# A two-block network on one core: down units prepared inside the last up chunk, small halves added early, twelve modulation products moved

## Chip, cores and metric

The kernel runs on one core of one Trainium2 chip. The metric is the device time of one launch in microseconds.

## What is computed

Two transformer-like blocks run one after the other on 256 tokens of width 2048 in float32. The first has attention and a state-space mixer, the second an RWKV-7 mixer (a recurrence over time, `_wkv7_scan`) and a pooling mixer. Each block ends in a feed-forward part, and each is steered by six modulation vectors:

```python
mod = silu(c) @ w_ada[l] + b_ada[l]              # 6 x 2048 values
x = x + gate_m * (mixer(h) @ w_out[l])
h = rms_norm(x) * (1 + scale_f) + shift_f
u = causal_dwconv(h @ w_up[l])                   # 2048 -> 2 x 5632, 3 taps
x = x + gate_f * ((silu(g) * val) @ w_down[l])   # 5632 -> 2048
```

## The kernel before

**Weights in units.** All large weights come in units of 128x2048 float32 (1 MB) through a ring of four slots. SyncE (SP) issues the load into `w_raw` (`load_w`), ScalarE (ACT) rounds the unit to a high part `w_hi` (`hi`, `hi_unit`), VectorE (DVE) subtracts to get the low part `w_lo` (`lo`, `lo_unit`), and TensorE (PE) multiplies high by high, high by low and low by high. A slot is refilled when PE has finished the unit four places back (`units_used`). Every engine runs its instructions in the order in which the code lists them, and semaphores join the engines; no scheduler moves anything.

**Two forms of the product.** `wide` (L750, L752) does a pair of matmuls: the high weight against 512 columns (high and low part of the input side by side, so that the two results lie in two halves of a bank), then the low weight against 256 columns into the second half. `three` (L745 to L747) does three matmuls of 256 columns into one half. With `wide` the sum of a bank's halves is taken later, by DVE.

**Feed-forward.** It is cut in two parts, A and B. Each has `up` chunks (12 or 10, of four units) and then a `down` phase (24 or 20 units). At the end of an up chunk a chain runs over ACT and DVE: `small` (ACT copies the second halves, L1308), `add` (DVE, L1974), `taps` (ACT L1314, DVE L1981), `silu` (ACT L1320), `product` (DVE L1991), `upper` (ACT L1324), `rest` (DVE L1995). In the middle of a phase this chain alternates with the preparation of the next chunk's units. After the last chunk, units 0 and 1 of the down phase are prepared ahead, the whole chain runs, and only then do units 2, 3 and so on follow (`stream` on ACT, `finish` on DVE, then `down`). There are four such ends: A and B in each block (down phases d = 0 to 3).

**Down phase.** PE goes through the first half of the units for eight banks, DVE adds both halves of each bank to `x` (`down_add`: first halves L2004, second halves L2010), and PE goes through the second half of the units. The phases with a name (`mid`, d = 1, which ends the first block, and `end`, d = 3) end with two units that are kept in a memory of their own (`kept_hi`, `kept_lo`). PE takes them bank by bank, so that banks become final one after the other. DVE adds them to `x`, ACT squares them and DVE sums the squares (`add_square`, L2017). PE closes with three matmuls against ones (`sums`, L855 and L858) for the norm that follows.

**Modulation.** One product `ada` (L1672) multiplies a row block of 128x2048 by the broadcast input on DVE and sums it into one column of `mod`. There are 192. From the 33rd on, GpSimd (POOL) loads the blocks into two buffers, `ada_raw`, the next for a buffer when its product is done (L2258). The products stand in DVE's order between other work, at places written out by hand: the table `products` of `down`, `one_ada` elsewhere.

**The recurrence.** `wkv_pe`, `wkv_act`, `wkv_dve` do two heads' groups s = 0, 1 at a time, in four passes i = 0 to 3. Near the end of a pass stand four rounds q, one for each chunk of 64 tokens. In a round PE multiplies by the state, DVE forms `rhs` (L1594), PE solves (L684), ACT copies `u` (L1084), and PE forms the state's increment (L695, L696). DVE has scaled the old state meanwhile (`state_w`, L1600) and now forms the new `state` (L1604), for which PE's next round waits. In passes 0 and 1 PE does a quarter of a weight unit in each round; in passes 2 and 3 it has nothing else there.

Of the kernel before, what the change touches and what calls it, by code (L numbers as in the profile page):

```python
# [16 lines left out]
ALU = mybir.AluOpType  # L17
# [152 lines left out]
def build_program(nc, a, out):  # L170
    with ExitStack() as ctx:
# [559 lines left out]
        def _(pe):  # L731
# [66 lines left out]
            def down(d, u0, hc0, e_next, n, name=None):  # L798
# [26 lines left out]
                for q in range(2, n):  # L825
# [5 lines left out]
                    for k, b in enumerate(banks):  # L831
# [280 lines left out]
        def _(act):  # L1112
# [49 lines left out]
            def stream(u0, e0, c0, c1, evac, u_next, ahead=True):  # L1162
# [5 lines left out]
                hi(0, 0, u_next)  # L1168
                if ahead:
                    hi(0, 1, u_next)  # L1170
                for f in evac:
                    f(c1 - 1, (e0 + c1 - 1) % 2)
                if not ahead:
                    hi(0, 1, u_next)
# [166 lines left out]
            def down(d, u0, n, e_next, u_next=None, name=None, joint=0):  # L1341
                banks, per = down_banks(e_next), n // 2
                for q in range(2, n if name is None else n - 4):
# [53 lines left out]
            hi(0, 0, U_DN1A)  # L1397
            hi(0, 1, U_DN1A)
            for f in ev:
                f(11, (UP1A + 11) % 2)  # L1400
# [70 lines left out]
        def wkv_dve(dve, steps, lo_unit, evac, add_half, i):  # L1471
# [116 lines left out]
            for q in range(4):  # L1588
# [56 lines left out]
        def _(dve):  # L1645
# [66 lines left out]
            def finish(c, e0, evac, u_next, ahead=True):  # L1712

                lo(0, 0, u_next)
                if ahead:
                    lo(0, 1, u_next)
                for f in evac:
                    f(c, (e0 + c) % 2)
                if not ahead:
                    lo(0, 1, u_next)  # L1720

            def stream(u0, e0, c0, c1, evac, p0, pairs, u_next=None, ahead=True):
# [36 lines left out]
                if u_next is not None:  # L1759
                    finish(c1 - 1, e0, evac, u_next, ahead)  # L1760
# [237 lines left out]

            def down_add(d, gate0, k, banks):
                for e in (k, k + 1):  # L2000
                    dve.wait_ge(down_tile, 16 * d + e + 1)
                    b = banks[e % 8]
                    j = 8 * (e // 8) + b
                    stt(out=x[:, j], in0=ps[:, b, 0:T], scalar=mod[:, gate0 + j:gate0 + j + 1], in1=x[:, j], op0=ALU.mult,  # L2004
                        op1=ALU.add).then_inc(down_half, 1)
                for e in (k, k + 1):
                    dve.wait_ge(down_half, 16 * d + e + 1)
                    b = banks[e % 8]
                    j = 8 * (e // 8) + b
                    stt(out=x[:, j], in0=ps[:, b, T:512], scalar=mod[:, gate0 + j:gate0 + j + 1], in1=x[:, j], op0=ALU.mult,  # L2010
                        op1=ALU.add).then_inc(down_out, 1)
# [11 lines left out]
            def down(d, u0, n, gate0, p0, products, e_next, u_next=None, name=None, joint=0):  # L2023
                banks, per = down_banks(e_next), n // 2
                pair = p0
                for q in range(2, n - 2 if name is not None else n):
# [16 lines left out]
                elif u_next is not None:  # L2043
                    lo_unit(u_next)
                for k in range(8, 16, 2):
                    if name is not None and u_next is not None and k == 12:
                        lo_unit(u_next + 1)
                    down_add(d, gate0, k, banks)
                    if name is not None:
                        for e in (k - 2, k - 1):  # L2050
                            if e >= 8:
# [337 lines left out]
```

## Time and profile before

| | |
|---|---|
| median of 3 runs | 2575.4 us (2571.93 to 2576.75) |
| profiled execution | 2577.89 us |
| its span in the trace | 2576.2 us |
| mean granted PE clock | 0.967 of full |
| PE busy | 2395.2 us, 93% of the span |
| DVE busy | 1948.6 us, 76% |
| ACT busy | 1176.8 us, 46% |

The span is the time from the first to the last recorded instruction. Busy shares are means over stages that are limited by different things; what matters for this change is what PE waits for at a few places, and at which of its two clock levels it works after them.

### The profile page before, as it was taken

To read this page: it belongs to the slowest core of one execution; us is meant where nothing else is said; L and a number is where in the kernel's file an instruction comes from. 1 tells how busy PE (TensorE), PEld (TensorE's weight loads), DVE (VectorE), ACT (ScalarE), POOL (GpSimd) and SP (SyncE) were. 2 spreads that over 40 slices of the span, in tenths; PEclk is the share of its full clock that TensorE was granted. 3 is DMA by queue.
4 is the path that set the end of the run, shared out by engine and by line. 5 is a ranking of instruction groups with operands and counts; after the bars stand their busy time and mean duration, and the time that the engine had idled before them with its cause. 6 is when DMAs were issued, how large, how long until landed. Compare 5 with 4: busy or idle time off the path is not lost.

```text
span 2576.2 us, 42584 instructions
## 1 busy us (share of the span) xinstructions
PE 2395.2 (93%) x17274; PEld 2148.4 (83%) x17274; DVE 1948.6 (76%) x2310; ACT 1176.8 (46%) x1290; POOL 96.1 (4%) x184
## 2 busy tenths in 40 slices
PE   4899958899999999999899889999899999999997
PEld 4899838888888888887699788889788888888886
DVE  6988878888797788878788576668888655566655
ACT  3344364355553345543444344434565543455442
POOL 0020000000000000000000000000000000000000
PEclk8999979999999999999999999889999999999999
DMA  8988956767777887768578122218576545555552
GB/s 358 421 332 323 341 182 252 303 259 279 280 298 298 330 304 275 272 260 341 189 270 318 67 89 97 95 58 305 227 279 258 187 172 193 183 185 190 180 213 97
DMA packets 88529, 615.76 MB, mean 239 GB/s; under 512 B 9656, under 2 KB 13264, under 8 KB 14928
## 3 DMA queue, kind: packets, MB, share of 16 engines
q1 hardware_dynamic: 65216, 445.07, 46.4%
q0 software_dynamic: 23184, 168.83, 17.5%
q8 instruction: 98, 1.61, 0.3%
q14 instruction: 31, 0.25, 0.0%
HBM read 609.64 MB, written 4.22 MB: 238 GB/s over the span
## 4 chain that ended last, share of the span: by engine, by line
PE 72%; DVE 15%; DMA 5%; ACT 5%; issue 2%; SPq 0%; DVEq 0%; POOLq 0%; ACTq 0%
PE ps L750 35%; PE ps L752 18%; PE ps L745 4%; PE ps L746 4%; PE ps L747 4%; DMA ada_raw<-in_ada_stream 2%; DVE w_lo L1660 2%; DVE ada_raw L1672 2%; DVE first_raw L1672 2%; DMA w_raw<-in_w_stream 1%; ACT w_hi L1128 1%; DMA first_raw<-in_ada_stream 1%; DVE w_lo L1656 1%; PE ps L631 1%; DVE conv_y L1981 1%
## 5 line engine op out<-in xcount | busy, mean ns | idle before, releaser
L750 PE MATMUL ps<-h_both,w_hi 128*128 128x512 f32 x2816 | 991.2, 396 | 15.3 <-DVE h_both L1703 14.4
L752 PE MATMUL ps<-h_both,w_lo 128*128 128x256 f32 x2816 | 791.9, 281 | 0.0
L750 PEld LDWEIGHTS ps<-h_both,w_hi 128*128 128x128 f32 x2816 | 530.4, 188 | 141.9 <-issue 16.7
L1656 DVE TENSOR_TENSOR w_lo<-w_raw,w_hi 128x2048 fp32r<-128x2048 f32 x225 | 513.6, 2287 | 98.9 <-ACT w_hi L1122 98.6
L1122 ACT CAST w_hi<-w_raw 128x2048 fp32r<-128x2048 f32 x226 | 430.6, 1911 | 256.3 <-DMA w_raw<-in_w_stream 243.3
L745 PE MATMUL ps<-h_both,w_hi 128*128 128x256 f32 x1664 | 485.8, 292 | 60.4 <-DVE h_both L1801 33.1
L752 PEld LDWEIGHTS ps<-h_both,w_lo 128*128 128x128 f32 x2816 | 534.6, 190 | 0.0
L750 PE MATMUL ps<-hid_both,w_hi 128*128 128x512 f32 x1344 | 472.6, 394 | 15.2 <-DVE w_lo L1660 15.2
L746 PE MATMUL ps<-h_both,w_hi 128*128 128x256 f32 x1664 | 477.1, 287 | 0.0
L747 PE MATMUL ps<-h_both,w_lo 128*128 128x256 f32 x1664 | 476.5, 286 | 0.0
L1660 DVE TENSOR_TENSOR w_lo<-w_raw,w_hi 128x2048 fp32r<-128x2048 f32 x147 | 335.4, 2288 | 130.8 <-ACT w_hi L1128 130.3
L1128 ACT CAST w_hi<-w_raw 128x2048 fp32r<-128x2048 f32 x146 | 277.0, 1907 | 322.8 <-DMA w_raw<-in_w_stream 320.9
L1672 DVE SCALAR_TENSOR_TENSOR ada_raw<-ada_raw,ada_c 128x2048 f32<-128x2048 f32 x160 | 365.3, 2284 | 36.5 <-DMA ada_raw<-in_ada_stream 36.5
L745 PEld LDWEIGHTS ps<-h_both,w_hi 128*128 128x128 f32 x1664 | 325.4, 196 | 69.6 <-DVE h_both L1801 35.2
L752 PE MATMUL ps<-hid_both,w_lo 128*128 128x256 f32 x1344 | 381.4, 284 | 0.0
L746 PEld LDWEIGHTS ps<-h_both,w_hi 128*128 128x128 f32 x1664 | 325.7, 196 | 0.5
L747 PEld LDWEIGHTS ps<-h_both,w_lo 128*128 128x128 f32 x1664 | 325.5, 196 | 0.0
L750 PEld LDWEIGHTS ps<-hid_both,w_hi 128*128 128x128 f32 x1344 | 255.0, 190 | 71.2 <-issue 17.2
L752 PEld LDWEIGHTS ps<-hid_both,w_lo 128*128 128x128 f32 x1344 | 256.7, 191 | 0.0
L1981 DVE SCALAR_TENSOR_TENSOR conv_y<-tmp,par,conv_y 128x254 f32<-128x254 f32 (+1 forms) x352 | 146.4, 478 | 13.7 <-ACT conv_y L1314 8.6
L2258 POOL DMA_DIRECT2D ada_raw<-in_ada_stream x160 | 84.6, 529 | 1702.2 <-DVE ada_raw L1672 1674.1
L1974 DVE TENSOR_TENSOR tmp<-ps,tmp 128x1024 f32<-128x1024 f32 x44 | 53.9, 1224 | 115.2 <-ACT tmp L1308 115.2
(355 smaller groups left out, 1823.6 us busy)
## 6 DMA issues: line engine op xcount, KB each, us to landing
w_raw<-in_w_stream SPq DMA_DIRECT2D x372, 1024.0 KB, 4.9
ada_raw<-in_ada_stream POOLq DMA_DIRECT2D x160, 1024.0 KB, 6.9
first_raw<-in_ada_stream SPq DMA_DIRECT2D x32, 1024.0 KB, 10.1
kept_raw<-in_w_stream SPq DMA_DIRECT2D x4, 1024.0 KB, 9.5
x<-in_x_t SPq DMA_DIRECT2D x1, 2048.0 KB, 10.0
cs_b<-cs_rows SPq DMA_DIRECT2D x4, 512.0 KB, 8.1
x_kept<-x SPq DMA_DIRECT2D x1, 2048.0 KB, 13.5
out_t<-x SPq DMA_DIRECT2D x4, 512.0 KB, 2.6
```

Source lines behind the costliest of these rows:

```text
L745: mm(o, hi, r_hi, start=first, stop=False, **kw)
L746: mm(o, hi, r_lo, start=False, stop=False, **kw)
L747: return mm(o, lo, r_hi, start=False, stop=last, **kw)
L750: mm(ps[:, b, :].rearrange("p (a t) -> p a t", a=2), hi, both[:, :, k], start=first, stop=False, skip_group_check=True)
L752: return mm(ps[:, b, T:512], lo, big[:, k], start=False, stop=False, skip_group_check=True)
L1122: nc.scalar.copy(w_hi[:, slot], w_raw[:, slot]).then_inc(hi_ready, 1)
L1128: nc.scalar.copy(w_hi[:, u % 4], w_raw[:, u % 4]).then_inc(hi_ready, 1)
L1656: tt(w_lo[:, slot], w_raw[:, slot], w_hi[:, slot].bitcast(F32), ALU.subtract).then_inc(lo_ready, 1)
L1660: tt(w_lo[:, u % 4], w_raw[:, u % 4], w_hi[:, u % 4].bitcast(F32), ALU.subtract).then_inc(lo_ready, 1)
L1672: stt(out=rows, in0=rows, scalar=1.0, in1=ada_c[:], op0=ALU.mult, op1=ALU.mult, accum_out=col(mod, pair)).then_inc(ada_done, 1)
L1981: last = stt(out=conv_y[:, par_, i, d:T], in0=tmp[:, i, 0:T - d], scalar=pc(par_name, o + 2 - d), in1=conv_y[:, par_, i, d:T], op0=ALU.mul ...
L2258: G.dma_start(ada_raw[:, slot], src).then_inc(ada_loaded[slot], 16)
```

## The change

It has three parts, and PE's, ACT's and DVE's orders are written anew in each.

1. **Ends of the up phases.** Down units 2 and 3 (`hi_unit` and `lo_unit` of `u_next + 2` and `u_next + 3`) now stand within the chain of the last chunk (`up_end`, `finish`), and the loops of `down` begin at unit 4. The products at q = 2 and 3 go elsewhere: phase 0 has its 18 at q = 4 to 11 and 14 to 23 (before 2 to 10 and 15 to 23), phase 1 has 6 (before 12).
2. **Kept units.** The second halves of the banks are final after the last streamed unit: DVE adds them to `x` then, and PE multiplies the kept units with `three`, which uses the first half alone. One half per bank is left for DVE behind the last matmuls, and the second of the next stage's units is prepared after all of it.
3. **Products.** Six products from phase 1 and six from the first RKV chunks go into the recurrence, one in each of the rounds q = 0, 1, 2 of the four passes.

```diff
 PE, down():
                         if q in (per - 1, n - 1):
                             last.then_inc(down_tile, 1)
+                        if name is not None and q == n - 3 and k < 7:
+                            last.then_inc(S(name + "_small"), 1)
...
-                    pairs = [weights(n - 2), weights(n - 1)]
-                    for b in banks:
-                        for q, (w_h, w_l) in enumerate(pairs):
-                            last = tile(b, w_h, w_l, 2 * (per - 2 + q), False)
+                    kept = [weights(n - 2), weights(n - 1)]
+                    for k, b in enumerate(banks):
+                        pe.wait_ge(down_half, 16 * d + 8 + k + 1)
+                        for q, (w_h, w_l) in enumerate(kept):
+                            for f in range(2):
+                                w, j = slice(f * 1024 + b * P, f * 1024 + b * P + P), 2 * (per - 2 + q) + f
+                                last = three(bank(b), w_h[:, w], w_l[:, w], hid_hi[:, j], hid_lo[:, j], False, False,
+                                             skip_group_check=True)
                         last.then_inc(down_tile, 1)
 ACT, end of an up phase:
+            def up_end(c, par_, ev, u_next):
+                hi_unit(u_next)
+                hi_unit(u_next + 1)
+                ev[0](c, par_)
+                hi_unit(u_next + 2)
+                ev[1](c, par_)
+                hi_unit(u_next + 3)
+                ev[2](c, par_)
+                ev[3](c, par_)
 DVE, a round of the recurrence:
                     steps.add(ts(state_w[s][:], state[s][:], wc[s][:, q:q + 1], None, ALU.mult))
+                one_ada(WKV_ADA - 15 + 3 * i + q)
                 steps.settle()
 DVE, end of an up phase:
-                lo(0, 0, u_next)
-                if ahead:
-                    lo(0, 1, u_next)
-                for f in evac:
-                    f(c, (e0 + c) % 2)
+                par_ = (e0 + c) % 2
+                lo_unit(u_next)
+                lo_unit(u_next + 1)
+                evac[0](c, par_)
+                lo_unit(u_next + 2)
+                evac[1](c, par_)
+                evac[2](c, par_)
+                lo_unit(u_next + 3)
+                evac[3](c, par_)
 DVE, down():
-                for q in range(2, n - 2 if name is not None else n):
+                for q in range(4, n - 2 if name is not None else n):
...
+                    for k, b in enumerate(banks):
+                        if k < 7:
+                            dve.wait_ge(S(name + "_small"), k + 1)
+                        else:
+                            dve.wait_ge(units_used, u0 + n)
+                        half_add(gate0, 8 + b, b, T).then_inc(down_half, 1)
+                    if u_next is not None:
+                        lo_unit(u_next)
+                    for k, b in enumerate(banks):
+                        dve.wait_ge(down_tile, 16 * d + 8 + k + 1)
+                        dve.wait_ge(down_half, 16 * d + 8 + k + 1)
+                        half_add(gate0, 8 + b, b, 0).then_inc(down_out, 1)
+                        if k >= 2:
+                            add_square(name, joint, 8 + k - 2)
+                    if u_next is not None:
                         lo_unit(u_next + 1)
 DVE, calls:
-            down(0, U_DN1A, 2 * FFN_A, GATE_F, 104, {**{q: 1 for q in range(2, 11)}, **{q: 1 for q in range(15, 24)}}, UP1B, U_UP1B)
+            down(0, U_DN1A, 2 * FFN_A, GATE_F, 104, {q: 1 for q in range(4, 24) if q not in (12, 13)}, UP1B, U_UP1B)
-            down(1, U_DN1B, 2 * FFN_B, GATE_F, 142, {2: 1, 3: 2, 4: 1, 5: 1, 6: 1, 7: 1, 8: 1, 14: 1, 15: 1, 16: 1, 17: 1}, C_LORA, U_LORA,
+            down(1, U_DN1B, 2 * FFN_B, GATE_F, 142, {4: 1, 6: 1, 8: 1, 14: 1, 16: 1, 17: 1}, C_LORA, U_LORA,
```

DVE's order at the end of the last up chunk of part B of the first block, from the preparation of down units 0 and 1 (`w_lo`) on, before:

```order
571 L1656 TENSOR_TENSOR w_lo<-w_raw,w_hi 128x2048 x2
572 L1974 TENSOR_TENSOR tmp<-ps,tmp 128x1024
573 L1981 SCALAR_TENSOR_TENSOR conv_y<-tmp,par,conv_y 128x255 x4
574 L1981 SCALAR_TENSOR_TENSOR conv_y<-tmp,par,conv_y 128x254 x4
575 L1991 TENSOR_TENSOR prod<-silu_g,conv_y 128x512
576 L1995 TENSOR_TENSOR hid_both<-prod,hid_both 128x512
577 L1683 TENSOR_TENSOR mod<-mod,par 128x32
578 L1708 SCALAR_TENSOR_TENSOR gain<-mod,par 128x16
579 L2095 TENSOR_TENSOR gain<-gain,par 128x16
580 L1660 TENSOR_TENSOR w_lo<-w_raw,w_hi 128x2048
581 L1672 SCALAR_TENSOR_TENSOR ada_raw,mod<-ada_raw,ada_c 128x2048
```

and after:

```order
559 L1668 TENSOR_TENSOR w_lo<-w_raw,w_hi 128x2048 x2
560 L1984 TENSOR_TENSOR tmp<-ps,tmp 128x1024
561 L1668 TENSOR_TENSOR w_lo<-w_raw,w_hi 128x2048
562 L1991 SCALAR_TENSOR_TENSOR conv_y<-tmp,par,conv_y 128x255 x4
563 L1991 SCALAR_TENSOR_TENSOR conv_y<-tmp,par,conv_y 128x254 x4
564 L2001 TENSOR_TENSOR prod<-silu_g,conv_y 128x512
565 L1668 TENSOR_TENSOR w_lo<-w_raw,w_hi 128x2048
566 L2005 TENSOR_TENSOR hid_both<-prod,hid_both 128x512
567 L1691 TENSOR_TENSOR mod<-mod,par 128x32
568 L1716 SCALAR_TENSOR_TENSOR gain<-mod,par 128x16
569 L2111 TENSOR_TENSOR gain<-gain,par 128x16
570 L1668 TENSOR_TENSOR w_lo<-w_raw,w_hi 128x2048
```

Units 2 and 3 have moved from behind the chain into it, and the next `w_lo` (row 570) is unit 4's.

DVE's order in the first two rounds of pass 0 of the recurrence, before:

```order
781 L1594 TENSOR_TENSOR rhs<-ps,tmp 64x128
782 L1594 TENSOR_TENSOR rhs<-ps,tmp_b 64x128
783 L1600 TENSOR_SCALAR state_w<-state,wc 128x64 x2
784 L1604 SCALAR_TENSOR_TENSOR state<-ps,wc,state_w 128x64 x2
785 L1594 TENSOR_TENSOR rhs<-ps,tmp 64x128
786 L1594 TENSOR_TENSOR rhs<-ps,tmp_b 64x128
```

and after:

```order
748 L1601 TENSOR_TENSOR rhs<-ps,tmp 64x128
749 L1601 TENSOR_TENSOR rhs<-ps,tmp_b 64x128
750 L1607 TENSOR_SCALAR state_w<-state,wc 128x64 x2
751 L1680 SCALAR_TENSOR_TENSOR ada_raw,mod<-ada_raw,ada_c 128x2048
752 L1612 SCALAR_TENSOR_TENSOR state<-ps,wc,state_w 128x64 x2
753 L1601 TENSOR_TENSOR rhs<-ps,tmp 64x128
```

One modulation product now stands between the scaled state and the new state.

DVE's order at the end of phase 1, with the additions to `x`, the sums of squares (`silu_g`) and the preparation of the next stage's units (`w_lo`), before:

```order
620 L2004 SCALAR_TENSOR_TENSOR x<-ps,mod,x 128x256 x2
621 L2010 SCALAR_TENSOR_TENSOR x<-ps,mod,x 128x256 x2
625 L1660 TENSOR_TENSOR w_lo<-w_raw,w_hi 128x2048
626 L2004 SCALAR_TENSOR_TENSOR x<-ps,mod,x 128x256 x2
627 L2010 SCALAR_TENSOR_TENSOR x<-ps,mod,x 128x256 x2
628 L2017 TENSOR_TENSOR silu_g<-silu_g,conv_y 128x512 x2
```

and after:

```order
593 L2010 SCALAR_TENSOR_TENSOR x<-ps,mod,x 128x256 x8
594 L1668 TENSOR_TENSOR w_lo<-w_raw,w_hi 128x2048
595 L2010 SCALAR_TENSOR_TENSOR x<-ps,mod,x 128x256 x3
605 L2010 SCALAR_TENSOR_TENSOR x<-ps,mod,x 128x256
606 L2025 TENSOR_TENSOR silu_g<-silu_g,conv_y 128x512
607 L1668 TENSOR_TENSOR w_lo<-w_raw,w_hi 128x2048
```

Eight additions (row 593) stand ahead of everything that waits for the kept units; behind the last bank one addition and one sum are left, and a unit's preparation follows them.

## Rows read from the trace of the kernel before

**Rows 1.** The page: busy times; PE's busy tenths and granted clock in 40 slices

```profile
PE 2395.2 (93%) x17274; PEld 2148.4 (83%) x17274; DVE 1948.6 (76%) x2310; ACT 1176.8 (46%) x1290; POOL 96.1 (4%) x184
...
PE   4899958899999999999899889999899999999997
...
PEclk8999979999999999999999999889999999999999
```

**Rows 2.** Timeline of PE: start, duration, instruction, idle time before it and its releaser

```profile
798.62 0.47 PE L750 MATMUL ps<-hid_both,w_hi 128*128 128x512 f32 x1 [3.12 <-DVE w_lo L1660]
...
1177.60 0.47 PE L750 MATMUL ps<-hid_both,w_hi 128*128 128x512 f32 x1 [1.24 <-DVE w_lo L1660]
```

**Rows 3.** Stretches: PE, PEld, DVE, ACT, POOL busy, granted clock, DMA share, GB/s

```profile
2093.20:2100.00 6.80, 5.71 (x18) 4.88 (x19) 6.80 (x4) 4.04 (x3) 0.00 (x0) 0.50 0.33 137
...
1274.00:1277.40 3.40, 3.39 (x4) 1.51 (x5) 0.00 (x0) 1.03 (x1) 0.00 (x0) 0.50 0.00 0
...
795.50:922.46 126.96, 123.84 (x705) 109.38 (x704) 102.92 (x87) 44.35 (x24) 9.50 (x18) 0.99 0.90 335
...
1160.30:1257.40 97.10, 91.15 (x513) 79.95 (x513) 80.10 (x67) 42.22 (x36) 6.33 (x12) 0.98 0.85 327
...
2091.16:2219.20 128.04, 124.90 (x705) 110.29 (x704) 63.34 (x51) 44.98 (x25) 0.00 (x0) 0.97 0.52 186
...
2457.06:2548.90 91.84, 88.80 (x512) 78.75 (x513) 49.73 (x41) 35.21 (x26) 0.00 (x0) 1.00 0.49 179
```

**Rows 4.** Timeline of ACT, then DVE, around the end of part B's last up chunk

```profile
1145.45 1.91 ACT L1122 CAST w_hi<-w_raw 128x2048 fp32r<-128x2048 f32 x1 [3.54 <-DMA w_raw<-in_w_stream]
...
1159.02 1.90 ACT L1128 CAST w_hi<-w_raw 128x2048 fp32r<-128x2048 f32 x1
...
1161.02 2.29 DVE L1660 TENSOR_TENSOR w_lo<-w_raw,w_hi 128x2048 fp32r<-128x2048 f32 x1 [0.66 <-ACT w_hi L1128]
...
1165.44 2.29 DVE L1660 TENSOR_TENSOR w_lo<-w_raw,w_hi 128x2048 fp32r<-128x2048 f32 x1
```

**Rows 5.** Timeline of PE, then DVE, at the ends of phases 1 and 3

```profile
1274.01 1.22 PE L855 MATMUL ps<-silu_g,ones 128*128 128x512 f32 x1 [5.34 <-DVE silu_g L2017]
...
2562.40 0.48 PE L855 MATMUL ps<-silu_g,ones 128*128 128x256 f32 x1 [2.22 <-DVE silu_g L2017]
...
1272.48 1.48 DVE L2017 TENSOR_TENSOR silu_g<-silu_g,conv_y 128x512 f32<-128x512 f32 x2
...
1259.01 0.48 DVE L2004 SCALAR_TENSOR_TENSOR x<-ps,mod,x 128x256 f32<-128x256 f32 x1 [6.09 <-PE ps L752]
```

**Rows 6.** Timeline of PE in a stretch of `three` at full clock

```profile
49.67 0.28 PE L745 MATMUL ps<-h_both,w_hi 128*128 128x256 f32 x1
...
50.63 0.28 PE L747 MATMUL ps<-h_both,w_lo 128*128 128x256 f32 x1
```

**Rows 7.** Timeline of DVE in rounds of pass 0, then of pass 2

```profile
1459.12 0.40 DVE L1600 TENSOR_SCALAR state_w<-state,wc 128x64 f32<-128x64 f32 x2
...
1461.82 0.47 DVE L1604 SCALAR_TENSOR_TENSOR state<-ps,wc,state_w 128x64 f32<-128x64 f32 x2 [2.30 <-PE ps L696]
...
1629.20 0.28 DVE L1604 SCALAR_TENSOR_TENSOR state<-ps,wc,state_w 128x64 f32<-128x64 f32 x1 [0.57 <-PE ps L696]
...
1631.70 0.62 DVE L1604 SCALAR_TENSOR_TENSOR state<-ps,wc,state_w 128x64 f32<-128x64 f32 x2 [0.58 <-PE ps L696]
...
1634.66 0.28 DVE L1604 SCALAR_TENSOR_TENSOR state<-ps,wc,state_w 128x64 f32<-128x64 f32 x1 [1.15 <-PE ps L696]
```

**Rows 8.** Stretches: the rounds of pass 0, and the slow spell of pass 2

```profile
1458.00:1474.00 16.00, 14.86 (x254) 12.85 (x249) 7.22 (x22) 2.38 (x9) 0.00 (x0) 1.00 0.03 6
...
1632.40:1649.50 17.10, 15.88 (x144) 11.99 (x143) 9.53 (x17) 7.55 (x14) 0.00 (x0) 0.50 0.19 62
```

**Rows 9.** Chain of work in phase 1: start, duration, piece

```profile
1167.80 5.12 DMA ada_raw<-in_ada_stream
...
1187.64 9.56 DMA ada_raw<-in_ada_stream
```

More of the change, by code:

```diff
@@ L1342, in down @@
                 banks, per = down_banks(e_next), n // 2
-                for q in range(2, n if name is None else n - 4):
+                for q in range(4, n if name is None else n - 4):
                     hi_unit(u0 + q)
@@ L1396, in _ @@
             chunk_runs(act, 9, 12, UP1A, up_body(U_UP1A, ev))
[L1397 to L1400, printed above, removed]
+            up_end(11, (UP1A + 11) % 2, ev, U_DN1A)
             down(0, U_DN1A, 2 * FFN_A, UP1B, U_UP1B)
@@ L1469, in _, with wkv_dve @@
             root(8)
[L1471 removed]
+        def wkv_dve(dve, steps, lo_unit, evac, add_half, one_ada, i):
             V = nc.vector
@@ L1710, in gains_of, with finish, stream @@
                 return [gain[:, k:k + 1] for k in range(KT)]
-            def finish(c, e0, evac, u_next, ahead=True):
-                lo(0, 0, u_next)
-                if ahead:
-                    lo(0, 1, u_next)
-                for f in evac:
-                    f(c, (e0 + c) % 2)
-                if not ahead:
-                    lo(0, 1, u_next)
-            def stream(u0, e0, c0, c1, evac, p0, pairs, u_next=None, ahead=True):
+            def finish(c, e0, evac, u_next):
+                par_ = (e0 + c) % 2
[7 more added lines that the diff above has]
+                evac[3](c, par_)
+            def stream(u0, e0, c0, c1, evac, p0, pairs, u_next=None):
                 def some_ada(c, i, odd):
@@ L1997, in hidden, with half_add @@
                 return (add, taps, product, rest)
+            def half_add(gate0, j, b, t0):
+                return stt(out=x[:, j], in0=ps[:, b, t0:t0 + T], scalar=mod[:, gate0 + j:gate0 + j + 1], in1=x[:, j], op0=ALU.mult,
+                           op1=ALU.add)
             def down_add(d, gate0, k, banks):
@@ L2001, in down_add @@
                     dve.wait_ge(down_tile, 16 * d + e + 1)
[L2002 to L2005, printed above, removed]
+                    half_add(gate0, 8 * (e // 8) + banks[e % 8], banks[e % 8], 0).then_inc(down_half, 1)
                 for e in (k, k + 1):
                     dve.wait_ge(down_half, 16 * d + e + 1)
[L2008 to L2011, printed above, removed]
+                    half_add(gate0, 8 * (e // 8) + banks[e % 8], banks[e % 8], T).then_inc(down_out, 1)
             def add_square(name, n, k):
@@ L2042, in down @@
                     lo(0, 0, u_next)
[L2043 to L2046, printed above, removed]
-                        lo_unit(u_next + 1)
[L2048 to L2051, printed above, removed]
-                                add_square(name, joint, e)
-                if name is None:
-                    lo(0, 1, u_next)
+                    for k in range(8, 16, 2):
+                        down_add(d, gate0, k, banks)
+                    lo(0, 1, u_next)
+                else:
+                    for k, b in enumerate(banks):
+                        if k < 7:
+                            dve.wait_ge(S(name + "_small"), k + 1)
+                        else:
+                            dve.wait_ge(units_used, u0 + n)
[9 more added lines that the diff above has]
+                    if u_next is not None:
+                        lo_unit(u_next + 1)
                 dve.wait_ge(down_out, 16 * d + 16)
@@ L2166, in first_add @@
                 add_half(j)
-            pair = 154
+            pair = 148
             lo_unit(U_LORA + 2)
@@ L2191, in _ @@
                 lo_unit(U_RKV + 2 * n + 2)
-                one_ada(pair + 7 + 2 * n)
                 lo_unit(U_RKV + 2 * n + 3)
                 rkv_evac(0, n)
-                one_ada(pair + 8 + 2 * n)
                 if n == 1:
```

12 lines of the change are left out of this document (4 added, 8 removed).

## Prediction

> **What bounds the kernel now.** I read the page first: PE is busy 93% of the span, 181 us short of it, and works at or near full clock in nearly all slices [rows 1]. So the time is PE's work, plus the places where PE waits, plus what PE loses at the lower of its clock levels. I then listed PE's idle stretches in the timeline and looked, for each place that the change touches, at what ended them.
>
> *Ends of the up phases.* At each of the four ends PE does down units 0 and 1 and then waits for unit 2: 3.12 us at phase 0 [rows 2], the same within 0.01 at phases 1 and 2, and 91.84 - 88.80 = 3.04 at phase 3 [rows 3]. The releaser is DVE's `w_lo`. Unit 2 is late because ACT begins it only when the chain of the last chunk is over: its cast starts at 1159.02, the subtraction ends at 1161.02 + 2.29 = 1163.3, and PE goes on there [rows 4]. After these waits the granted clock is 0.50 for a while; the longest such spell is the 6.8 us at 2093.2, over the end of the wait of phase 2 [rows 3]. The cost of both shows in whole phases. Phase 3, which has no slow spell, needs 88.80 us of PE for its 16 units behind the wait, 5.55 each [rows 3]. At that rate phases 0 and 2 (22 units) would take 122.1, and phase 1 (16 units) 88.8; from the start of the wait they take 126.96, 128.04 and 97.10, and phase 3 takes 91.84 [rows 3]. The excess is 4.9 + 5.9 + 8.3 + 3.0 = 22.1 us. In phase 1 it holds further waits of PE for `w_lo`, 1.24 us at 1177.60 the first [rows 2]: DVE stands there before a product whose block is still on its way, with transfers of 5.12 to 9.56 us on the chain [rows 9].
>
> *Ends of phases 1 and 3.* PE waits 5.34 us and 2.22 us between the last kept matmul and `sums`, for DVE's additions and sums of squares [rows 5]. A clock of 0.50 lies on the first `sums` [rows 3].
>
> *The recurrence.* In pass 0 DVE idles 2.30 us in a round between `state_w` and `state`, waiting for PE, which has a quarter of a unit to do. In pass 2 it idles 0.57, 0.58 and 1.15 us in the three rounds [rows 7]. The chain PE, DVE, PE, ACT, PE, DVE is closed there: what DVE is late, PE is late.
>
> **Part 1, up to down.** The same casts and subtractions in another place; the question is only whether they fit. Loads come one per unit time in this stage: ACT got unit 1's at 1145.45, after waiting 3.54 us for it [rows 4], so unit 2's is there by about 1145.45 + 5.55 = 1151.0 and unit 3's by 1156.6. With 1.91 on ACT and 2.29 on DVE unit 2 is ready near 1155.3, and PE wants it at 1163.46 - 3.13 = 1160.3. Unit 3 waits for `product` on DVE, which two inserted subtractions push back by about 1.5 us to 1159.9; it is ready near 1162.3 and wanted at 1160.3 + 5.55 = 1165.9. What is late next is the chain itself (`rest` ends near 1163), and it is wanted only at the last unit of the first half, seven or more units on. Unit 4's load is issued as before, and ACT is free for it earlier. So all four waits go, and with them, I take it, the slow spells that follow them. The further waits of phase 1 go too: its products stand every second unit (4, 6, 8), so a block has 11 us to arrive, more than the longest 9.56 [rows 9]. In phase 0 two products move past units 10 and 14; DVE spends 2.2 + 2.2 of each 5.55 us there, so they hide behind PE, at a margin that the additions at unit 13 narrow. If that cover fails, one product costs 2.2. Of 22.1 us I take 21.5, with 12.4 (the four waits alone, no clock back) as the lower bound and 22.1 as the upper.
>
> **Part 2, kept units.** Behind the last kept matmul DVE has one addition (0.48, [rows 5]) and one sum (half of the 1.48 for two, 0.7) left, about 1.2 us with the hand-over; the second half is out of the way, since DVE idles 6.09 us in front of the first addition [rows 5], room for the eight early ones. So 5.34 becomes 1.2, and at phase 3, where the sum is over half as many columns, 2.22 becomes 1.0: a gain of 4.1 and 1.2. The next stage's second unit (2.29) is behind them on DVE and hides under `sums`. With a wait of 1.2 instead of 5.3 us the clock should still be up at `sums`; the spell of 3.4 us at 0.50 [rows 3] is worth at most 1.7, I take 1.2, and 0 as the other bound. Against this, PE's kept work is dearer: 32 sets of three matmuls per phase in place of 32 pairs. Three go at 0.36 us (eight starts in 0.96, [rows 6]), a pair at 88.80 / 256 = 0.347 [rows 3], so 0.4 to 0.5 more per phase. Part 2 brings 4.1 + 1.2 + 1.2 - 1.0 = 5.5, between 3.5 and 6.5.
>
> The Trainium skill prices the same edit lower: "TensorE: Matmul & The Clock Gate", section Back-to-back issue gap, gives N / 2.4 ns + 2.5 ns for an isolated matmul, by which three of 256 cost only 2.5 ns more than 512 and 256, or 0.08 us per phase. By that estimate part 2 would bring 6.3. The rows of `three` are slower per column than this formula, so I stay with the rows.
>
> **Part 3, products.** Six leave phase 1 (counted above). Six leave the RKV chunks, in the slices from 1288 to 1417 us, where PE is at nine tenths or more [rows 1]; I cost their leaving at nothing. Twelve enter rounds. A product between two instructions of DVE takes 1165.44 - 1163.31 = 2.13 us [rows 4].
>
> Passes 0 and 1: the idle time of 2.30 us [rows 7] holds 2.13. Cost 0, under cover of PE's quarter unit. Uncovered, each would cost 2.13.
>
> Passes 2 and 3: DVE's wait becomes 2.13, which is 1.56, 1.55 and 0.98 us later in the three rounds [rows 7]. From the second on about 0.23 comes back, because both groups' states then follow each other at once (0.47 for two in pass 0 against 0.28 each and a wait between). That is 3.9 per pass, 7.7 for both, if pass 3, whose code is the same here, has the same waits.
>
> The blocks: the first two of a pass are in the buffers, the third's load is issued when the first product is done. A round of pass 2 is 1631.70 - 1629.20 = 2.50 us now and 2.50 + 1.55 - 0.23 = 3.8 then, which leaves two rounds less a product, 2 x 3.8 - 2.3 = 5.3 us, for a load that takes at least 5.12 [rows 9], plus the time until POOL issues it. In passes 0 and 1 the rounds are about as long. I take 0.4 us of waiting in each pass, 1.6 in all; with 9.56 [rows 9] it would be some 4.7 each. DMA is nearly idle there (share 0.03, [rows 8]), which is why I stand near the low end.
>
> The clock: passes 2 and 3 already have a slow spell from their rounds on, 17.1 us at 0.50 in pass 2, while the rounds of pass 0, with weight work in them, ran at 1.00 [rows 8]. Longer waits of PE in the rounds can only start that earlier or hold it longer. A spell of 3.4 us more costs up to 1.7; I take 1.4 in all, between 0 and 7.
>
> Together 7.7 + 1.6 + 1.4 = 10.7, between 8 and 25.
>
> **Sum.** 21.5 + 5.5 - 10.7 = 16.3 us faster. The profiled execution took 2577.89, its span 2576.2, so that one would become 2561.6. It lies 2.5 above the median of 2575.4, which becomes 2559. What a measurement of this kernel can tell from no change is about 0.2%, 5 us.
>
> **Rivals.**
> *The clock is not given back, or units stay late* (0.14). The slow spells belong to another rhythm, or unit 3 or 4 becomes the late one. Phase 3 had its wait without a slow spell, which speaks for it; that phase 2's spell begins at 2093.2, 2 us into the wait that opens its row of 128.04 us speaks against. Part 1 brings 12.4 to 16: 2565 to 2568.
>
> *The rounds are dearer* (0.13). Loads of 7 to 9 us, or several more slow spells in passes 2 and 3. Part 3 costs 16 to 22: 2564 to 2570. The Trainium skill speaks for this one: "TensorE: Matmul & The Clock Gate", section HAM oscillation, tells of a kernel in which waits of PE between short bursts of matmuls dropped the clock again and again.
>
> *It does nothing on balance* (0.05). The third product of each pass waits for a load of 9.56 us: 4 x 4.7 = 18.8 in place of 1.6, so part 3 costs 28 against 27 gained, 2575. Only overlapping transfers made loads that long.
>
> *Slower* (0.05). The products do not fit into the rounds of passes 0 and 1 either: state and product then queue, each of the twelve costs its whole 2.13 plus the wait for its turn, near 2.5, 30 us, and PE's waits take the clock down in passes 0 and 1 as in pass 2, four spells of 1.7, 7 more. 37 - 27 gives 2585. It decides from a cost of 27 us for part 3, 2.25 for each product. The 2.30 us of idle time [rows 7] speak against it.
>
> **How the numbers follow.** The forecast's own range is 2554 to 2564 (part 1 at 19 to 22, part 2 at 4 to 6.5, part 3 at 8.5 to 13), chance 0.63. The range of 8 in 10 goes from 2553 to 2568: it takes in most of the first two rivals. Faster by over 0.2% (below 2570.2) holds the forecast and nearly all of the first two rivals, 0.88; within 0.2% holds the third and the rest of them, 0.07; slower 0.05.
>
> **What would show each step.** Right: no wait of PE over 0.3 us between units 1 and 2 of any down phase, and phases that go through at 5.55 us a unit and a clock of 1.00; 1.0 to 1.3 us in front of `sums`; DVE's idle time in the rounds of passes 0 and 1 near 0.1, and these rounds no longer than before; rounds of passes 2 and 3 longer by 1 to 1.6 us, with the third product waiting some tenths for its block. Wrong: `w_lo` of unit 3 or 4 as releaser of PE; a clock of 0.50 early in a down phase; rounds of passes 0 and 1 longer by over 0.3 us; `ada_raw` on the chain with waits of microseconds in the recurrence.

## The result and the profile after

| | before | after |
|---|---|---|
| median | 2573.66 us (2570.94 to 2576.75, 4 runs) | 2551.24 us (2546.60 to 2552.09, 4 runs) |
| profiled execution | 2577.89 us | 2550.66 us |
| its span | 2576.2 us | 2549.0 us |
| mean granted PE clock | 0.967 | 0.972 |

The ratio is 0.9909, with a 95% interval from 0.9891 to 0.9927: some 22 us faster. The prediction had 2559.0 and a range of 2553 to 2568. The direction was right. The gain was taken too small, and the median lies just under the range. One of six executions of the changed kernel that were timed later took 3915.78 us at a mean clock of 0.555, and no ratio below counts it.

The page of the changed kernel, busy times and PE's slices, answers to [rows 1]:

```profile
PE 2378.1 (93%) x17338; PEld 2136.7 (84%) x17338; DVE 1948.1 (76%) x2310; ACT 1176.9 (46%) x1290; POOL 96.0 (4%) x184
...
PE   4899958899999999999899888889899999999997
...
PEclk8999989999999999999999999889999999999999
```

PE has 64 matmuls more (`three` on the kept units) and is busy 17.1 us less: what it gained is partly time at a higher clock. The bound has not changed.

**Ends of the up phases.** Stretches of the changed kernel (busy time of PE, PEld, DVE, ACT, POOL, granted clock, DMA share, GB/s), each from the first matmul of unit 2 to the end of a down phase, in the order of phases 0 to 3. They answer to [rows 3], which begin with the wait before that matmul:

```profile
798.49:921.09 122.60, 122.19 (x707) 108.10 (x705) 98.60 (x84) 42.09 (x22) 9.50 (x18) 1.00 0.90 345
1158.39:1247.13 88.74, 88.74 (x514) 78.67 (x513) 65.55 (x63) 39.91 (x34) 3.17 (x6) 1.00 0.77 292
2078.49:2201.11 122.62, 122.18 (x706) 108.09 (x705) 61.26 (x53) 43.06 (x23) 0.00 (x0) 1.00 0.54 195
2434.16:2522.91 88.75, 88.75 (x515) 78.68 (x514) 50.49 (x48) 32.87 (x24) 0.00 (x0) 1.00 0.51 187
```

All four run at a clock of 1.00, and in phases 1 and 3 PE's busy time is the whole stretch: no wait is left. In phases 0 and 2 one wait of 0.4 us is left, in the middle of the phase, for DVE's additions to `x`. PE enters unit 2 without one (timeline of PE, no bracket behind a row), against 3.12 us in [rows 2]:

```profile
1158.27 0.28 PE L752 MATMUL ps<-hid_both,w_lo 128*128 128x256 f32 x1
1158.39 0.39 PE L750 MATMUL ps<-hid_both,w_hi 128*128 128x512 f32 x1
```

The timeline of DVE over the same chain, which answers to [rows 4]:

```profile
1150.34 2.29 DVE L1668 TENSOR_TENSOR w_lo<-w_raw,w_hi 128x2048 fp32r<-128x2048 f32 x1 [0.58 <-ACT w_hi L1134]
...
1157.22 2.28 DVE L1668 TENSOR_TENSOR w_lo<-w_raw,w_hi 128x2048 fp32r<-128x2048 f32 x1
...
1162.79 2.29 DVE L1668 TENSOR_TENSOR w_lo<-w_raw,w_hi 128x2048 fp32r<-128x2048 f32 x1 [2.16 <-ACT w_hi L1134]
```

Unit 2 is ready at 1152.6 and wanted at 1158.39. Unit 3 is ready at 1159.5 and wanted 5.55 later, at 1163.9. Both have more than 4 us to spare. For unit 4 DVE waits 2.16 us again, for ACT and the load, and still ends well ahead of PE.

**Kept units.** The timeline of PE at the two `sums`, which answers to [rows 5]:

```profile
1259.67 1.12 PE L861 MATMUL ps<-silu_g,ones 128*128 128x512 f32 x2 [1.18 <-DVE silu_g L2025]
1260.64 1.88 PE L864 MATMUL ps<-conv_y,ones 128*128 128x512 f32 x4
1267.99 0.55 PE L745 MATMUL ps<-h_both,w_hi 128*128 128x256 f32 x1 [5.48 <-DVE h_both L1711]
...
2535.18 0.70 PE L861 MATMUL ps<-silu_g,ones 128*128 128x256 f32 x2 [0.91 <-DVE silu_g L2025]
```

The waits are 1.18 and 0.91 us instead of 5.34 and 2.22. From the first matmul of `sums` to the first of the next stage it is 1267.99 - 1259.67 = 8.32 us. The kernel before needs 1284.00 - 1274.01 = 9.99, since it works there at 0.50 of the clock [rows 3]; the end of its stretch in the timeline of PE:

```profile
1284.00 0.55 PE L745 MATMUL ps<-h_both,w_hi 128*128 128x256 f32 x1 [5.48 <-DVE h_both L1703]
```

**The rounds.** The timeline of DVE in the first round of pass 0 and the third round of pass 3, which answers to [rows 7]:

```profile
1443.32 2.28 DVE L1680 SCALAR_TENSOR_TENSOR ada_raw<-ada_raw,ada_c 128x2048 f32<-128x2048 f32 x1
1445.53 0.07 DVE L1680 DVE_READ_ACCUMULATOR ada_raw<-ada_raw,ada_c 128x1 f32 x1
1445.71 0.48 DVE L1612 SCALAR_TENSOR_TENSOR state<-ps,wc,state_w 128x64 f32<-128x64 f32 x2
...
1706.12 0.40 DVE L1607 TENSOR_SCALAR state_w<-state,wc 128x64 f32<-128x64 f32 x2
1707.95 2.29 DVE L1680 SCALAR_TENSOR_TENSOR ada_raw<-ada_raw,ada_c 128x2048 f32<-128x2048 f32 x1 [1.44 <-DMA ada_raw<-in_ada_stream]
```

In pass 0 the product fills the idle time of 2.30 us and `state` follows at once. In pass 3 the third product waits 1.44 us for its block. The chain of work shows why: the load of that block took 6.50 us.

```profile
1701.42 6.50 DMA ada_raw<-in_ada_stream
```

The load issued in pass 3 once its first product is done took 6.3 to 6.5 us in the profiles of `after`, `after_again`, `rounds23` and `ten_rounds`, and 5.1 us in `part3_only`; all others in the rounds took 4.9 to 5.7. What makes it long was not found out.

From the first `rhs` of the first round to that of the fourth, the four passes took 11.96, 11.97, 8.09 and 8.09 us before, and 12.03, 12.10, 12.33 and 13.66 us after.

### The profile page after: what moved, and what is told of

It is laid out like the page before. It is cut to its first block, busy times and chain, and to the rows that moved or that the text cites. A ratio compares the mean times of both kernels' runs of the same rounds, so it can differ in the third digit from the quotient of the medians.

```text
span 2549.0 us, 42730 instructions
## 1 busy us (share of the span) xinstructions
PE 2378.1 (93%) x17338; PEld 2136.7 (84%) x17338; DVE 1948.1 (76%) x2310; ACT 1176.9 (46%) x1290; POOL 96.0 (4%) x184
## 3 DMA queue, kind: packets, MB, share of 16 engines
HBM read 609.64 MB, written 4.22 MB: 241 GB/s over the span
## 4 chain that ended last, share of the span: by engine, by line
PE 75%; DVE 13%; DMA 6%; ACT 4%; issue 2%; SPq 0%; DVEq 0%; POOLq 0%; ACTq 0%
PE ps L750 37%; PE ps L752 19%; PE ps L745 4%; PE ps L747 4%; PE ps L746 4%; DMA ada_raw<-in_ada_stream 2%; DMA w_raw<-in_w_stream 2%; DVE first_raw L1680 2%; DVE ada_raw L1680 2%; DVE w_lo L1668 2%; DMA first_raw<-in_ada_stream 1%; ACT w_hi L1134 1%; PE ps L631 1%; DVE w_lo L1664 1%; DVE xbc L1830 1%
## 5 line engine op out<-in xcount | busy, mean ns | idle before, releaser
L750 PE MATMUL ps<-hid_both,w_hi 128*128 128x512 f32 x1344 | 466.1, 390 | 0.0
L1680 DVE SCALAR_TENSOR_TENSOR ada_raw<-ada_raw,ada_c 128x2048 f32<-128x2048 f32 x160 | 365.3, 2285 | 27.2 <-DMA ada_raw<-in_ada_stream 27.0
```

The lines of the kernel that those rows point to most:

```text
L750: mm(ps[:, b, :].rearrange("p (a t) -> p a t", a=2), hi, both[:, :, k], start=first, stop=False, skip_group_check=True)
L1680: stt(out=rows, in0=rows, scalar=1.0, in1=ada_c[:], op0=ALU.mult, op1=ALU.mult, accum_out=col(mod, pair)).then_inc(ada_done, 1)
```

## Experiments

My theory after the result was that the parts add up: part 1 gives what was said, part 2 more, part 3 costs less than said. The rivals were a part 1 that gives much more (the clock given back beyond the phases), a part 3 that costs nothing, and a mere difference between executions. Ratios are to the kernel before on the same chip, each with its 95% interval.

**Each part alone.** `part1_only`: the kernel before with `up_end`, the new `finish` and both loops of `down` from unit 4. Its twelve products of phase 1 stay there:

```diff
-            down(1, ..., 142, {2: 1, 3: 2, 4: 1, 5: 1, 6: 1, 7: 1, 8: 1, 14: 1, 15: 1, 16: 1, 17: 1}, C_LORA, U_LORA,
+            down(1, ..., 142, {**{q: 1 for q in range(4, 10)}, **{q: 1 for q in range(12, 18)}}, C_LORA, U_LORA,
```

> The kernel before with part 1 alone: units 2 and 3 inside the last chunk's chain; phase 1 keeps its twelve products, at q = 4 to 9 and 12 to 17. Theory (the waits and the slow spells behind them were the cost): PE goes from unit 1 to unit 2 without a wait in all four phases, no clock of 0.50 in a down phase, and the time is 20 to 23 us under the kernel before. Rival (only the waits go, the clock does not come back): 12 to 16 us under it.

Measured: 0.9910 (0.9891 to 0.9929), 2553.5 us: 23 us under the kernel before, which is the theory's upper end. All four waits and the spells behind them are gone. Its stages account for 18.7 us of it (table below).

`parts12`: the changed kernel without a product in the rounds. The six of the RKV chunks are back in their places, and phase 1 has its twelve as above.

```diff
-                one_ada(WKV_ADA - 15 + 3 * i + q)
...
+                one_ada(pair + 7 + 2 * n)
...
+                one_ada(pair + 8 + 2 * n)
```

> The changed kernel without part 3: no product in the rounds, twelve in phase 1 and six in the RKV chunks. Theory (part 3 costs about 10 us in the rounds, and the rest of its difference is spells of the clock that come and go between runs): 7 to 11 us under the changed kernel, 28 to 32 under the kernel before. Rival (the products in the rounds cost only 3 to 4 us net, because they also take slow spells away in the recurrence): 2 to 5 us under the changed kernel, 24 to 27 under the kernel before.

Measured: 0.9908 (0.9889 to 0.9927), 2550.9 us. That is 23.7 us under the kernel before and no less than the changed kernel's 0.9909, so the theory's 28 to 32 and 7 to 11 us did not come. The number is nearest to the rival's, but its reason is not shown by it: 4.2 us, what part 3 costs in all by the stages below, are less than the half width of the interval, 4.9 us.

`part3_only`: the kernel before with twelve products in the rounds, six fewer in phase 1 and six fewer in the RKV chunks.

> The kernel before with part 3 alone: twelve products in the rounds, six in phase 1 (q = 2, 4, 6, 14, 16, 17), none in the RKV chunks. Theory: slower than the kernel before by about 7 us (10 in the rounds, 3 back in phase 1, where the products no longer wait for blocks). Rival (part 3 takes slow spells away): no difference or faster.

Measured: 1.0023 (1.0007 to 1.0039), 2580.8 us: part 3 costs time by itself, about 6 us. The prediction has 10.7 us for part 3 and counts the relief of phase 1 with part 1. Less the 1.7 us by which phase 1 got shorter here, 9.0 us are left, a ratio of 1.0035, which is still inside the interval. So this time alone does not refute the 10.7.

`three_only`: the kernel before, the kept units multiplied with `three` and nothing else.

```diff
-                            last = tile(b, w_h, w_l, 2 * (per - 2 + q), False)
+                            for f in range(2):
+                                ...
+                                last = three(bank(b), w_h[:, w], w_l[:, w], hid_hi[:, j], hid_lo[:, j], False, False,
+                                             skip_group_check=True)
```

> The kernel before with one edit: PE multiplies the kept units with three matmuls of 256 columns into the first half in place of a pair of 512 and 256; DVE's work is as before. My pricing by rows of another stage: 0.4 to 0.5 us more in each of phases 1 and 3, a kept stretch of 11.7 us in place of 11.27. Rival (same columns, same time): 11.3 to 11.4 us. In the time of the whole kernel neither is to be seen.

Measured: 0.9984 (0.9969 to 1.0000). By its kept stretches it should be 0.2 us slower than the kernel before, 1.0001, just outside this interval; whether that is chance stayed open. The time cannot price `three`, but the trace can. The stretch of the kept matmuls in the kernel before, then in this one:

```profile
1257.42:1268.67 11.25, 11.25 (x66) 9.72 (x64) 7.63 (x13) 3.06 (x8) 0.00 (x0) 1.00 0.35 129
```

```profile
1258.57:1269.93 11.36, 11.36 (x98) 11.15 (x96) 7.69 (x13) 3.05 (x8) 0.00 (x0) 1.00 0.38 138
```

That is 0.11 us per phase, where the prediction had 0.48.

`part2_only`: the changed kernel with parts 1 and 3 undone.

> Before with part 2 alone. If the stages of the earlier profiles add up (wait before `sums` 5.34 to 1.2 and 2.2 to 0.9, `sums` of the first block at full clock, `three` on the kept units costing 0.1 per phase), it is faster by about 7 us, ratio 0.9973. By the prediction's terms (`three` costing 0.5 per phase) it is 5.5, ratio 0.9979. A rival in which the gain in front of `sums` is given back in the next stage has 0 to 3 us, ratio 0.999 to 1.000. The waits at the ends of the up phases (3.1 us) must stay.

Measured: 0.9978 (0.9960 to 0.9996), 2568.4 us. Its wait before `sums` is 1.17 us and the stretch to the next stage is 8.32 us, as in the changed kernel. By its stages it should bring 7.2 us (below), a ratio of 0.9972; the prediction's 5.5 would be 0.9979. The ratio allows both.

**Where the products cost.** `rounds01`: the changed kernel with products in the rounds of passes 0 and 1 alone; the six others are back in the RKV chunks. `rounds23`: the same with passes 2 and 3 instead.

```diff
+                if i < 2:
+                    one_ada(WKV_ADA - 9 + 3 * i + q)
```

> The changed kernel with products only in the rounds of passes 0 and 1 (six), the other six back in the RKV chunks. Theory (a product costs nothing where PE has a quarter of a unit to do, and all of part 3's price lies in passes 2 and 3): rounds of passes 0 and 1 as long as before, and 8 to 11 us under the changed kernel. Rival (the products cost in passes 0 and 1 too, or the RKV chunks miss their room): under 5 us below it.

> The changed kernel with products only in the rounds of passes 2 and 3 (six), the other six back in the RKV chunks. Theory (all of the price lies in passes 2 and 3): the time of the changed kernel within 2 us. Rival (half of the price lies in passes 0 and 1, or in the RKV chunks): 4 us or more off it.

Measured: 0.9875 (0.9845 to 0.9905) and 0.9921 (0.9895 to 0.9947), 2546.0 and 2556.6 us. Against the changed kernel in the same comparison (0.9914) that is 10.0 us less and 1.8 us more, as both theories had it, though with intervals of 7 to 8 us to either side. The rounds of passes 0 and 1 take 12.03 and 12.11 us with products and 11.97 without; those of passes 2 and 3 take 12.28 and 13.69 in `rounds23` and 8.04 and 8.05 in `rounds01`.

In the same comparison stood the changed kernel and the kernel before once more.

> The changed kernel once more. Theory (spells of 0.50 of one step in the recurrence come and go between executions, and so does the pace of an up phase, 22.2 or 22.6 us a chunk): another set of single spells and another set of paces than in the first profile, with the rounds of passes 2 and 3 the same. Rival (both belong to the program): the same spells and the same paces.

> The kernel before once more. Theory (the lottery): fewer or more than the five single spells of 0.50 between 1400 and 1750 us, and up phases with another pace than in the first profile, where the first and third went at 22.2 us a chunk and the second and fourth at 22.6; the slow spells behind the waits at the ends of the up phases are there again. Rival (they belong to the program): the same five spells and the same paces.

Measured: 0.9914 (0.9884 to 0.9944) and 0.9992 (0.9971 to 1.0013). So the result repeats, and a difference of 2 us between two kernels is below what their times tell. Both theories hold. Between 1400 and 1750 us the kernel before had six spells of 3.4 us in its first profile and two in this one, the changed kernel one and three. The third up phase of the kernel before went at 22.2 us a chunk, then at 22.6, and so did the fourth of the changed kernel. The rounds of passes 2 and 3 took 12.5 and 13.5 us in the changed kernel, much as in its first profile (12.33 and 13.66).

`ten_rounds`: the changed kernel without the third product in passes 2 and 3; the two stand in the first RKV chunk.

```diff
-                one_ada(WKV_ADA - 15 + 3 * i + q)
+                if i < 2 or q < 2:
+                    one_ada(WKV_ADA - 13 + 3 * i + q - (i == 3))
```

> The changed kernel without the third product in the rounds of passes 2 and 3; those two products stand in the first RKV chunk instead. If the third product's load is a cost of its own in pass 3, the third round of pass 3 falls from 5.55 us to the 2.3 us of before, so pass 3's rounds take 10.0 us in place of 13.7; in pass 2, where the block came just in time, the round loses only its own product, so 12.3 becomes 10.5. Together 5 to 6 us less than the changed kernel. If only the product itself counted, each would give 1.6 us, 3 in all.

Measured: 0.9903 (0.9876 to 0.9930). Rounds of passes 2 and 3: 11.52 and 11.17 us, against 12.33 and 13.66. I had expected 10.5 and 10.0, from a third round of 2.3 us; the third round without a product takes 3.1 us, in the kernel before as well. The timeline of DVE in the third round of pass 3 of this kernel:

```profile
1700.04 0.40 DVE L1607 TENSOR_SCALAR state_w<-state,wc 128x64 f32<-128x64 f32 x2
1701.59 0.67 DVE L1613 SCALAR_TENSOR_TENSOR state<-ps,wc,state_w 128x64 f32<-128x64 f32 x2 [1.16 <-PE ps L696]
```

From the third round to the fourth it is 3.06 us here, 4.22 in pass 2 of the changed kernel (the product alone, 1.2 more) and 5.55 in pass 3 (1.3 more, which is the load). Together the rounds are 3.3 us shorter, not 5 to 6; that is the size of the other expectation, 3 us, although the load did count in pass 3. The stage from pass 2 to the next up phase, at 247.6 us, is only 1.2 us shorter than in the profile of the changed kernel.

**The best version.** `rounds01` and `parts12` once more, beside each other.

> The changed kernel with products only in the rounds of passes 0 and 1, once more, beside the next kernel. If a product in a round of passes 0 and 1 costs 0.1 us and six fewer products in phase 1 are worth 2 to 3 us, it is 1 to 2 us faster than parts 1 and 2 alone, ratio to before 0.990. If the six products cost their work somewhere else in the recurrence (its earlier profile had 528.8 us there against a mean of 522.4), it is 3 to 4 us slower than parts 1 and 2 alone, ratio 0.992 to 0.993.

> Parts 1 and 2 with no product in the rounds, once more, on the same chip as the kernel before it. Expected 24 us faster than before, ratio 0.9907, and within 2 us of the kernel with products in passes 0 and 1; the recurrence from the first block's norm to the next up phase takes 519 to 527 us as in the five earlier profiles without products in it.

Measured: 0.9892 (0.9864 to 0.9921), 2543.4 us, and 0.9904 (0.9878 to 0.9930), 2549.0 us. The first kernel is 3 us faster by these ratios, in the direction of the first expectation, though the intervals overlap and the first reaches 0.9921, where the rival begins. The rival's reason falls: the recurrence from the first block's norm to the next up phase took 528.8 us in the first profile of `rounds01` and 520.4 in this one, against 523.6 in `parts12_again`. What tells the two kernels apart is phase 1, from its first down matmul to the first kept one. It takes 103.13 us in `parts12`, 103.89 in `parts12_again`, and 99.84 and 99.85 in the two profiles of `rounds01`. Stretches of phase 1 in `parts12`, then in `rounds01`:

```profile
1147.89:1251.02 103.13, 100.57 (x578) 88.48 (x577) 86.89 (x86) 47.65 (x43) 6.34 (x12) 1.00 0.83 319
```

```profile
1143.80:1243.64 99.84, 99.84 (x578) 88.60 (x577) 74.08 (x74) 47.91 (x43) 3.18 (x6) 1.00 0.72 273
```

With twelve products PE idles 2.56 us in `parts12`, and DVE has 12.8 us more to do. The timeline of PE in `parts12_again`, and of DVE ahead of that wait:

```profile
1236.90 0.47 PE L750 MATMUL ps<-hid_both,w_hi 128*128 128x512 f32 x1 [1.65 <-DVE w_lo L1667]
```

```profile
1230.05 2.29 DVE L1679 SCALAR_TENSOR_TENSOR ada_raw<-ada_raw,ada_c 128x2048 f32<-128x2048 f32 x1
1232.26 0.08 DVE L1679 DVE_READ_ACCUMULATOR ada_raw<-ada_raw,ada_c 128x1 f32 x1
1232.26 2.29 DVE L2028 TENSOR_TENSOR kept_lo<-kept_raw,kept_hi 128x2048 fp32r<-128x2048 f32 x1
1234.47 2.28 DVE L1667 TENSOR_TENSOR w_lo<-w_raw,w_hi 128x2048 fp32r<-128x2048 f32 x1
```

DVE never idles here. For each of two streamed units it has a product, a kept unit and that unit to do, from 1230.05 to 1236.67, where the next such set begins, that is 6.6 us, and PE needs 5.55 for a unit. PE waits for the difference.

**The stages of all fourteen profiles.** Each number is the time from the first matmul of one stage to that of the next, as a mean over the profiles that have the same form there (in brackets their range and number). `ten_rounds`, which alone has four products in passes 2 and 3, is left out of the last row.

| stage | without the part | with it | gain |
|---|---|---|---|
| down phase 0 | 138.7 (137.1 to 140.0, 5 profiles) | 133.7 (8; the ninth has 134.8) | 5.0 |
| down phase 2 | 138.2 (137.0 to 139.7, 5) | 133.7 (9) | 4.5 |
| down phase 3 | 104.4 (103.1 to 104.7, 5) | 99.8 (9) | 4.5 |
| down phase 1, twelve products | 107.7 (106.9 to 108.4, 4) | 103.0 (101.9 to 103.9, 3) | 4.7 |
| down phase 1, six instead of twelve, with part 1 | 103.0 | 99.85 (6) | 3.1 |
| kept matmuls, waits, first `sums` to norm | 11.25, 5.34 and 2.22, 10.3 (10.0 to 11.0) | 11.36, 1.18 and 0.91, 8.32 | 7.2 |
| norm to pass 2 | 282.0 (280.3 to 284.4, 8) | 282.0 (280.9 to 285.4, 6) | 0.0 |
| pass 2 to the next up phase, six products | 241.1 (238.4 to 244.2, 9) | 248.4 (246.4 to 249.3, 4) | -7.3 |

Part 1 with the relief of phase 1 is 18.7 + 3.1 = 21.8 us, part 2 is 7.2, part 3 is -7.3: 21.7 in all. Read back as ratios on 2575 us, these terms give the list below; each lies within its interval.

| kernel | from the stages | measured |
|---|---|---|
| part 1 alone | 0.9927 | 0.9910 |
| part 2 alone | 0.9972 | 0.9978 |
| part 3 alone (phase 1 gains 1.7 in that form) | 1.0022 | 1.0023 |
| parts 1 and 2 | 0.9899 | 0.9908, 0.9904 |
| products in passes 2 and 3 | 0.9916 | 0.9921 |
| `ten_rounds` (247.6 us from pass 2 on, 6.5 more than without products) | 0.9913 | 0.9903 |
| all (the changed kernel) | 0.9916 | 0.9909, 0.9914 |
| products in passes 0 and 1 | 0.9887 | 0.9875, 0.9892 |

## Why the prediction was right and wrong

**Part 1: right in the mechanism; the size came out with some luck.** Predicted 21.5, measured 21.8 by the stages. All four waits went, and the spells at 0.50 with them. In each of the five profiles without part 1, three or four such spells lie behind the ends of up phases; in the nine with it, none does. The rival "the clock is not given back" is refuted by that. The luck is in the single phases. Phase 2 was to bring 5.9 us and phase 3 3.0, as one profile of the kernel before had them, with a double spell behind the one wait and none behind the other; over five profiles both are worth 4.5, and the two errors cancel. The relief of phase 1 is real too, but its cause is partly another one than I gave. I had argued with blocks that are on their way; with twelve products and part 1 it is DVE, full in the second half of the phase, that makes PE wait (`parts12_again`).

**Part 2: right in the mechanism, too small: 5.5 predicted, 7.2 by the stages.** The waits came out as said (4.16 and 1.31 for 4.1 and 1.2). Two terms were off, by 0.8 us each. One is the price of `three`: "Three go at 0.36 us ... a pair at 88.80 / 256 = 0.347, so 0.4 to 0.5 more per phase". It is 0.11. The two rates came from two stretches, and both were off: the kept stretch itself has 11.25 / 32 = 0.352 for a pair and 11.36 / 32 = 0.355 for three. The Trainium skill ("TensorE: Matmul & The Clock Gate", section Back-to-back issue gap) led to an estimate of 0.08 per phase, which the trace nearly confirms with 0.11; I had set it aside. It is the difference of the two forms that holds; a whole set, estimated by that formula of the Trainium skill at 0.33 us, takes longer in both. The other term is the clock at `sums`: 10.3 - 8.32 = 2.0 us in the mean for the 1.2 I took.

**Part 3: the rounds right, the sum too dear: 10.7 predicted, 7.3 measured.** Passes 0 and 1 were to cost nothing; their rounds grew by 0.1 us a pass, and the stage that holds them by 0.0. Passes 2 and 3 were to cost 7.7 plus 1.6 for loads, 9.3. In the four profiles with all six products they take 12.3 to 12.5 and 12.2 to 13.7 us, in the others 8.0 to 8.8: more in the mean by 4.1 and 5.1: 9.2. Within that the loads came differently than said: waits of at most 0.2 us in passes 0 to 2, and of 1.3 to 1.5 us in pass 3 in three profiles of four. The failed step is the term for the clock, "A spell of 3.4 us more costs up to 1.7; I take 1.4 in all": the stage was to grow by 1.4 us more than its rounds and grew by 1.9 less, by 7.3.

What the traces show in its place is where the low clock lies. From pass 2 to the next up phase PE is at 0.50 for 41.6 us in the mean with six products and for 35.8 without, so the spells did get longer. But 17.1 us of the 41.6 lie in the rounds themselves, where PE waits for DVE, against 7.7 us without products. Outside the rounds it is 24.5 us against 28.0, so less than before. And outside them a longer low clock goes with a longer stage. In the nine profiles without products there, the stage less its rounds takes from 221.6 us (`part1_only`, 20.0 us at 0.50 outside the rounds) to 228.1 us (`before`, 39.1 us). A straight line through the nine has 0.31 us for each us at 0.50 (correlation 0.97). By that line 3.5 us less of it are worth 1.1 of the 1.9 us. The rest is within the scatter: the four profiles with six products lie from 1.8 us under the line to 0.5 over it, and `ten_rounds` 0.4 under it. That the products caused the shift is not shown, since the ranges overlap (18.7 to 29.2 us against 20.0 to 39.1).

The Trainium skill ("TensorE: Matmul & The Clock Gate", section HAM oscillation) tells of a kernel whose clock fell in each wait between short bursts of matmuls, and which lost time by it. The trace agrees that waits in the rounds go with a longer low clock, 17.1 us for 7.7; that this made the whole stage dearer than its rounds, as the rival had it, the traces do not bear out.

**The sum.** 21.8 + 7.2 - 7.3 = 21.7 in place of 16.3. Of the 7.8 us between the predicted and the measured median these 5.4 are the larger part. The median of before moved by 1.7 with the fourth run, and the rest is scatter. The two profiled executions differ by 27.2 us, 5.5 more than the 21.7, by the scatter of single profiles: of the stages that no part should change, norm to pass 2 was 1.2 us and the up phases were 1.4 us shorter in the profile of after, and the stage from pass 2 on grew by only 4.6 us, because the profile of before had one of the slow ones there.

The range failed because the forecast's terms leaned to the same side: I took the dearer row for `three`, the dearer one for the clock in part 3 and the smaller gain at `sums`. Two of its sums are also slightly off. Its own terms for the forecast give 10 to 20 us of gain, 2555 to 2565 and not 2554 to 2564. And the 0.23 us that comes back "from the second on" is taken off once per pass; taken off for both rounds it gives 3.6 per pass, where pass 2, which had no wait for a load, grew by 4.1.

## What to carry to other kernels

Work of a vector engine costs nothing in a wait that is as long as the work, and its excess in a shorter one. Here six products were free in waits of 2.3 us and six cost 7 us in waits of 0.6 to 1.2 us. Putting only the first six into the rounds, and leaving the others in the RKV chunks, gave the best kernel by its stages, and by its times too (0.9875 and 0.9892), though the intervals overlap. When a wait at a stage's end goes, look at the clock after it as well: four waits of 3.1 us were worth 4.5 to 5.0 each, with a spell of 0.50 behind most of them. And price a changed form of an operation against the stretch in which it will stand, not against another stage's rows.

## What was not expected of the hardware

The same matmuls of an up phase go at one of two paces in an execution, both at a granted clock of 1.00 and with no wait of PE. Eight chunks of the last up phase, in the profile of before and in that of after:

```profile
2242.28:2423.18 180.90, 180.90 (x1026) 156.78 (x1025) 118.11 (x120) 94.08 (x88) 0.00 (x0) 1.00 0.52 186
```

```profile
2223.37:2400.86 177.49, 177.49 (x1026) 155.23 (x1025) 118.03 (x120) 93.62 (x88) 0.00 (x0) 1.00 0.52 189
```

That is 22.61 or 22.19 us per chunk, for code that is the same. Over the fourteen profiles each of the four up phases shows now the one and now the other, with no link to the kernel: a phase of ten chunks takes 221.9 or 226.2 us (once 227.3). The first phase often takes a time between its two. What decides it stayed open. Two profiles of one kernel differ by up to 8 us. The two of `rounds01` are 7.7 us apart; 4.3 us of that lie between norm and pass 2 and 4.1 from pass 2 on, so there it is the recurrence and not the paces. Both are why stages, not spans, had to be compared.
